# A weight's low part moved behind a norm's, and a weight's rounding ahead of a tanh

## The reference

```
x = first_block(...)                    # ends with a gated feed-forward and a final RMS norm
# second block, first stage
h = rms_norm(x, pre_mix_g)
z = h @ w_in                            # columns: za (gMLP), q, k, v (MoBA), zc (conformer convolution)
a, g = split(zc);  y = a * sigmoid(g)   # GLU, then a causal depthwise convolution of 31 taps
m = rms_norm(mem, mem_g);  k, v = split(m @ w_xkv)   # cross-attention keys and values
```

## Time and profile before

| | us |
|---|---|
| median of 3 runs | 747.65 (747.18 to 748.11) |
| profiled execution, its own time | 747.14 |
| span of the profiled execution | 745.4 |
| PE busy | 737.5 (99% of the span) |
| DVE busy | 532.4 (71%) |
| ACT busy | 408.0 (55%) |
| mean granted TensorE clock | 0.999 of full |

### The profile page before, as it was taken

How to read it: one execution, slowest core, us unless ns; L and a number is a source line. 1 busy time by engine, 2 the same in 40 slices (tenths; PEclk the granted TensorE clock), 3 DMA queues, 4 the chain that set the end, 5 groups by cost and what they waited for, 6 DMA issues and landing times. The chain is left out here.

```text
span 745.4 us, 9905 instructions
## 1 busy us (share of the span) xinstructions
PE 737.5 (99%) x4024; PEld 634.3 (85%) x4024; DVE 532.4 (71%) x628; ACT 408.0 (55%) x519; POOL 39.3 (5%) x69
## 2 busy tenths in 40 slices
PE   9999999999999999999999999999999999999996
PEld 9988888889988888888888897788987888888885
DVE  6888946885766666666789999786758655566564
ACT  6678378544545545444763585674647443454442
POOL 0200002120000000000200000020003000000000
PEclk9999999999999999999999999999999999999999
DMA  9966365554565456666466536364165566555531
GB/s 340 287 229 223 128 242 209 170 172 168 174 222 170 170 173 204 210 203 213 157 198 205 191 113 226 116 234 148 44 215 169 159 218 226 174 207 181 165 120 57
DMA packets 81373, 138.39 MB, mean 186 GB/s; under 512 B 3884, under 2 KB 42672, under 8 KB 81200
## 3 DMA queue, kind: packets, MB, share of 16 engines
q1 hardware_dynamic: 79472, 132.69, 53.2%
q10 hardware_dynamic: 1856, 5.06, 1.9%
HBM read 136.69 MB, written 1.05 MB: 185 GB/s over the span
## 5 line engine op out<-in xcount | busy, mean ns | idle before, releaser
L1334 DVE TENSOR_TENSOR low<-raw,high 128x2048 fp32r<-128x2048 f32 (+1 forms) x120 | 271.3, 2278 | 101.9 <-ACT high L702 96.3
L702 ACT ACTIVATE high<-raw 128x2048 fp32r<-128x2048 f32 (+3 forms) x134 | 234.6, 1769 | 108.2 <-PE wide L2120 84.5
L2120 PE MATMUL wide<-act_hl,high 128*128 128x512 f32 (+1 forms) x960 | 239.0, 364 | 0.3 <-DVE act_hl L1399 0.2
L2120 PEld LDWEIGHTS wide<-act_hl,high 128*128 128x128 f32 x960 | 171.0, 190 | 28.6 <-issue 0.5
L2120 PE MATMUL wide<-high,act_hl 128*128 128x512 f32 x528 | 170.1, 394 | 0.5 <-DVE act_hl L1431 0.3
L2120 PE MATMUL wide<-act_hl,low 128*128 128x256 f32 x832 | 160.1, 282 | 0.0
L2120 PEld LDWEIGHTS wide<-act_hl,low 128*128 128x128 f32 x832 | 127.6, 191 | 2.7 <-DVE low L1382 0.2
L2120 PEld LDWEIGHTS wide<-high,act_hl 128*128 128x128 f32 x528 | 99.1, 188 | 23.4 <-issue 1.5
L2120 PE MATMUL wide<-low,act_hl 128*128 128x512 f32 x264 | 102.9, 390 | 0.0
L702 ACT ACTIVATE arena<-wide 128x512 f32<-128x512 f32 x62 | 35.1, 596 | 94.5 <-PE wide L2120 94.3
L2120 PE MATMUL bank<-high,hid_hl 128*128 128x512 f32 x256 | 80.1, 389 | 0.0
(11 more groups left out here) (219 smaller groups left out, 698.6 us busy)
## 6 DMA issues: line engine op xcount, KB each, us to landing
raw<-in_w_ff_dram SPq DMA_DIRECT2D x32, 1024.0 KB, 5.4
raw<-in_w_in_dram SPq DMA_DIRECT2D x27, 1024.0 KB, 5.3
raw<-in_w_ffn_in_dram SPq DMA_DIRECT2D x40, 512.0 KB, 4.9
raw<-in_w_ffn_out_dram SPq DMA_DIRECT2D x11, 1024.0 KB, 6.9
raw<-in_w_xkv_dram SPq DMA_DIRECT2D x8, 1024.0 KB, 5.0
raw<-in_w_o_dram SPq DMA_DIRECT2D x4, 1024.0 KB, 5.0
raw<-in_w_out_dram SPq DMA_DIRECT2D x4, 1024.0 KB, 5.3
raw<-in_w_xq_dram SPq DMA_DIRECT2D x4, 1024.0 KB, 5.2
```

Source lines behind the costliest of these rows:

```text
L702: return act.activation(dst, src, func, **k)
L1334: tt(part(low, g), part(raw, g), f32(part(high, g)), SUB).then_inc(sem.low_by_dve, 1)
L2120: return pe.matmul(dst, lhs, rhs, start=start, stop=stop, skip_group_check=loose)
```

## The change

Two edits, both of order alone. No instruction is added or removed.

On ACT, the rounding of the weight group `q2 1` (`split_high` up to `zc 1` + 2) is called ahead of `zc_tanh`; the following `ahead_of(("zc", 1))` then finds it done.

On DVE, the low part of `zc 0` is made behind `half_total(k_mem[:, 0:2, :])` and `norm_split(2)` instead of ahead of both, and the low part of `zc 1` behind `half_total(k_mem[:, 2:4, :])` instead of ahead of it. The two lines `me.used += 1` and `me.pairs += 1` keep the counts that `ahead_of` kept.

```
@@ scalar engine
             ahead_of(("zc", 0), "H")
             kv_high(1)
             low_part(in2(cs))
+            split_high(chunks[("zc", 1)][0][0] + LEAD + 1)
             zc_tanh()
             ahead_of(("zc", 1), "H")
             low_part(in2(cx))
@@ vector engine
             add_acc()
             final_norm()
             scale_x()
-            ahead_of(("kv", 0, 0), "H")
+            me.used += 1
+            me.pairs += 1
             half_total(k_mem[:, 0:2, :])
             norm_split(2)
-            ahead_of(("kv", 0, 1), "H")
+            split_low(chunks[("kv", 0, 0)][0][0] + LEAD + 1)
+            me.used += 1
+            me.pairs += 1
             half_total(k_mem[:, 2:4, :])
+            split_low(chunks[("kv", 0, 1)][0][0] + LEAD + 1)
             k_mem_low(0)
             ahead_of(("zc", 0), "H")
             k_mem_low(1)
```

## The result

The changed kernel takes 753.8 us (median of 5 runs, 752.78 to 754.19) against 747.4 us (median of 5) before: ratio 1.0083, 95% interval 1.0068 to 1.0098, so 5.1 to 7.3 us slower. That lies in the range on record (751.0 to 753.8), at its upper end, and not at the forecast of 751.7: it is close to rival 1's 753.6. The profiled execution took 752.78 us (span 751.0), the shortest of the five.

The account below looks back on a forecast made before the run. PE, busy 99% of the span, was taken to bound the kernel, so its waits count. A delay of 4.28 less 0.23 gave +4.05 us, 747.65 + 4.05 = 751.7 us; range 751.0 to 753.8.

Parts of the forecast that it names:

- rival 1: PE's clock falls in the gap ahead of `zc 0` and returns slowly: +1.9 us, 753.6 in all; chance 0.26.
- PE waits for the weight's low part: Ahead of `zc 0`, the weight's low part, formerly ready 1.5 us early, becomes PE's last condition instead of the norm's.
- The working of the delay, +4.28: DVE makes `zc 0`'s low part after the norm's parts, so PE starts `zc 0` at 380.62 instead of 376.34: +4.28 us.
- Late next: nothing: Behind `zc 0`, low parts of `zc 1` and `q2 0` come in time and later DMAs stay hidden: no cost.
- Rivals 2 and 3: Norm's low parts still decide `zc 0`'s start, 747.15, chance 0.03; `q2 1`'s later transfer not hidden, say 752.7, chance 0.03.
- The ACT edit, -0.23: Rounding `q2 1` ahead of the tanh puts DVE's chain ahead, removing PE's wait ahead of `k2 0`: -0.23 us.
- The likeliest time, 751.7: Whole kernel: 747.65 + 4.05 = 751.7 us, the case without a clock fall; chance 0.64.
- The sum of 4.05: Delay at `zc 0` less the gain at `k2 0`: 4.28 - 0.23 = +4.05 us.
- The price of 1.9 us: Slow clock behind the gap: if it returns as slowly as it fell, half of 3.8 us is lost.

Follow-up runs that it names:

- e6: Changed kernel with the low part of `zc 0` behind the half sum but ahead of `norm_split(2)`: 747.50 us, ratio 0.9998.
- e5: Kernel before with only the low part of `zc 1` moved behind the second half sum: 747.57 us, ratio 1.0001.
- e1: Kernel before with the ACT edit alone (rounding of `q2 1` ahead of the tanh): 747.26 us, ratio 0.9993.
- e2: Changed kernel with the ACT edit undone, DVE's order alone: 753.11 us, ratio 1.0071.
- e3: Changed kernel with 18 unused matmuls of ones on PE in the gap ahead of `zc 0`: 752.13 us, ratio 1.0058.
- e4: Changed kernel with the low part of `zc 0` between the norm's second and third pair of low parts: 751.27 us, ratio 1.0051.
- e8: Changed kernel with the low part of `zc 0` behind the norm's first pair of low parts: 750.36 us, ratio 1.0034.
- e9: e4 with 11 unused matmuls of ones on PE in the gap: 750.17 us, ratio 1.0036.
- e7: Kernel before with the ACT edit and the low part of `zc 0` in three pieces, two ahead of `scale_x`'s instructions: 746.76 us, ratio 0.9989.

## Why the prediction was right, and where it was not

- *PE waits for the weight's low part, which the list of waits did not name.* Right, and shown: the releaser is that low part, and e6, which puts it ahead of the norm, takes the loss away.
- *The working of the delay, +4.28.* 4.20 in the trace. DVE idles 1.80 us for ACT (worked out 1.85), makes the norm's parts in 3.23 (3.22) and the low part in 2.28.
- *Late next: nothing.* Right as far as PE goes. The low parts of `zc 1` and `q2 0` and the later DMA let no matmul wait in the list, and e5 shows the move of `zc 1`'s to be free. The transfers did take longer than the 5.2 to 5.5 us of the working: those issued from 380.9 to 399.9 landed after 5.1 to 7.1 us, and stayed hidden. Rivals 2 and 3 are out.
- *The ACT edit, -0.23.* PE wins 0.34 there in e1's trace, as the first pair behind the wait had been slow too. In the changed kernel the wait is gone as well, but e2 loses it without the edit. So I credited the gain to the wrong part there: behind the gap the edit is worth nothing that its interval shows, and the time comes back in either case.
- *The likeliest time, 751.7, is the step that failed.* I gave the clock 0.26 and took the case without it as the likeliest. It fell in the profiled execution, and by their mean clocks in all five: 0.997 in the one that took 752.78 and 0.995 in the four that took 753.77 to 754.19, where the runs of before beside the experiments have 0.998 to 1.000, but for one of 0.997. The sum of 4.05 is about what remains when PE is kept at work (e3: +4.4, interval 3.4 to 5.3). The rest is the clock's: 1.57 us in the changed kernel's trace, where it stayed low for 3.4 us, and 2.3 in e2's, where it stayed low for 6.8. The four longer runs fit the second.
- *That the range held is owed to rival 1, and its exact price to luck.* The range reached to 753.8 only because it took in the clock's case. The price of 1.9 us came from the assumption that the clock comes back as slowly as it falls. It does not hold: the clock fell after 4.9 us and came back after 3.4 in the changed kernel, and after 2.6 and 6.8 in e2. That 753.6 lies so near 753.8 is chance; by the traces a fall cost 1.4 (e4), 1.6 (the changed kernel) and 2.3 us (e2).
- *Why I weighed it too low.* I read one row at the kernel's end (3.8 us) as if a fall needed about that long. e2 and e4 fell after 2.6 and 2.5 in the gap, and at the kernel's end alone the traces run from 2.1 us (e6, last matmul ended 740.47, fall at 742.6) to 5.3 (e3, 744.70 and 750.0). One row could not tell that. The Trainium skill (TensorE: Matmul & The Clock Gate, "HAM oscillation — how this bites in real kernels") says that a product behind an idle gap starts cold and that this is paid at each gap. e2 and e4 agree with it, with 0.77 and 0.78 us for the first pair of `zc 0` against 0.41 before. The changed kernel agrees in part, as its first pair took 0.42 and only the next ones were slow, and e8's profiled execution, with a gap of 2.2 us, paid nothing.

The end of e6 by stretches, with PEclk third from the right:

```profile
740.50:742.00 1.50, 0.00 (x0) 0.00 (x0) 1.03 (x3) 1.07 (x3) 0.00 (x0) 1.00 0.84 315
742.00:743.00 1.00, 0.00 (x0) 0.00 (x0) 0.93 (x4) 0.00 (x0) 0.00 (x0) 0.80 0.00 0
743.00:744.00 1.00, 0.00 (x0) 0.00 (x0) 0.71 (x2) 0.00 (x0) 0.00 (x0) 0.50 0.08 31
```

What stays open is the slower pace in the traces of e3, e4, e6, e8 and e9, and the 0.23 us that the changed kernel's profiled execution regained behind `k2 0`. Its largest step, 0.10 near 462 us, stands in the traces of all the other kernels against the one of before, so it is no effect of the gap.

## What to carry to other kernels

A list of waits names only the condition that ended last. Before a producer is moved behind another wait, list every condition of its consumer with the time at which each was met. Here the low part had 1.5 us to spare and was put behind a wait of 1.8 and work of 3.2. Work that does not depend on a wait belongs ahead of it.

In this kernel, whose PE never rests, a new gap of 2.9 or 4.4 us cost its length and then 1.4 to 2.3 us more for the clock, and one of 2.2 us did so in some executions by their mean clocks. So price the clock in whenever a gap comes to more than 2 us. Matmuls that nothing uses take that second part away (e9 against e4, e3 against the changed kernel).

## What the runs showed of the hardware

- After PE stopped in the middle of dense work, the granted clock fell 2.5 us (e4), 2.6 us (e2) and 4.9 us (the changed kernel) behind its last matmul, and did not fall in a profiled gap of 2.2 us (e8). At the kernel's end it fell 2.1 us (e6) to 5.3 us (e3) behind the last. It stayed low for 3.4 us (the changed kernel, 381.4 to 384.8; e4, 379.3 to 382.7) or 6.8 us (e2). By the mean clocks of the changed kernel's runs (0.997 once, 0.995 four times) one program gives either, which makes its times spread.
- At 1.2 GHz a pair of matmuls of 512 and 256 columns took 0.640 us instead of 0.347: 1.85 times as long, not twice.
- POOL's small instructions grow longer while DVE works on two inputs in SBUF. In e7 one of DVE's pieces ran from 370.17 to 370.85, and POOL's power beside it took 0.87 us, against 0.57 in the kernel before (at 369.73, with DVE idle). So the pieces delay the very factor that `scale_x` waits for, by 0.30 us each, and DVE's idle of 0.77 did not hold 0.68 us of work for nothing. PE lost nothing by it: its transposes of the scaled x start 3.04 us ahead of the last matmul of `kv 0,1` as before (373.47 and 376.51, against 372.78 and 375.82):

```profile
370.17 0.68 DVE L1426 TENSOR_TENSOR low<-raw,high 128x512 fp32r<-128x512 f32 x1
371.32 0.75 DVE L1434 TENSOR_SCALAR xn<-x,rstd 128x1024 f32<-128x1024 f32 x1 [0.46 <-POOL rstd L584]
...
370.42 0.87 POOL L584 TENSOR_TENSOR rstd<-var,neg_half 128x1 f32<-128x1 f32 x1
```

The Trainium skill (GPSIMD Engine Reference, "1. Specifications") has the two engines share their interface to SBUF and names instructions of DVE with two SBUF inputs as a cause of contention; the row agrees, with 0.30 us more. What another kind of DVE instruction would have done at this place was not tried.
